# Norm chains in pieces, and a new order of the second block's attention, modulation and output

## What is computed

```python
mod = jax.nn.silu(c) @ w_ada[l] + b_ada[l]
sh1, sc1, g1, sh2, sc2, g2 = jnp.split(mod, N_MOD, axis=-1)
h = rms_norm(x, norm1_g[l]) * (1.0 + sc1[:, None]) + sh1[:, None]
z = h @ w_in[l]                      # q, k, v (512 each) and u (512) for the pools
a_out = diff_attention(q, k, v, lam, subln_g[l], lambda_init)
p_out = multiscale_pool(u, w_pool[l], pool_scale[l])
mix = jnp.concatenate([a_out, p_out], axis=-1) @ w_out[l]
x = x + g1[:, None] * mix
h = rms_norm(x, norm2_g[l]) * (1.0 + sc2[:, None]) + sh2[:, None]
y = hierarchical_moe(h, ...)
x = x + g2[:, None] * y
return rms_norm(x, final_g)
```

## Time and profile before

| | |
|---|---|
| median of 3 runs | 2242.56 us (2238.19 to 2245.31) |
| span of the profiled execution | 2239.7 us |
| TensorE matmul busy | 2032.3 us, 91% |
| TensorE weight load busy | 1722.9 us, 77% |
| VectorE busy | 1202.3 us, 54% |
| ScalarE busy | 902.2 us, 40% |
| HBM read | 496.03 MB, 222 GB/s over the span |

### The profile page before, as it was taken

How to read it: one execution, slowest core, us unless ns; L and a number is a source line. 1 busy time by engine, 2 the same in 40 slices (tenths; PEclk the granted TensorE clock), 3 DMA queues, 4 the chain that set the end, 5 groups by cost and what they waited for, 6 DMA issues and landing times.

```text
span 2239.7 us, 47727 instructions
## 1 busy us (share of the span) xinstructions
PE 2032.3 (91%) x20606; PEld 1722.9 (77%) x20606; DVE 1202.3 (54%) x2113; ACT 902.2 (40%) x1088; POOL 30.9 (1%) x61
## 2 busy tenths in 40 slices
PE   8999999989999999999999999999897767777775
PEld 7998858889999989988588899999776533343433
DVE  4887856388677557878563886775233200000001
ACT  5554533474555455545334755554312200000001
POOL 0000000000000000000000000000000000000000
PEclk9999999999999999999999999999998898878878
DMA  6554333445445554553334454556662699999996
GB/s 254 183 204 178 132 113 133 160 160 189 169 178 187 202 196 175 208 184 132 114 132 160 160 182 165 182 188 226 249 242 94 276 421 422 422 422 422 422 422 259
DMA packets 70920, 499.45 MB, mean 223 GB/s; under 512 B 8320, under 2 KB 8448, under 8 KB 12016
## 3 DMA queue, kind: packets, MB, share of 16 engines
q1 hardware_dynamic: 66240, 481.41, 56.2%
q0 software_dynamic: 4384, 14.75, 1.9%
q10 hardware_dynamic: 144, 1.05, 0.1%
HBM read 496.03 MB, written 1.15 MB: 222 GB/s over the span
## 4 chain that ended last, share of the span: by engine, by line
PE 69%; DMA 14%; DVE 6%; ACT 5%; SPq 3%; issue 2%; DVEq 0%; ACTq 0%
PE bank L863 25%; PE bank L868 12%; DMA ring<-stream 11%; PE bank L873 9%; DMA arena<-stream 4%; SPq L715 3%; PE bank L1102 3%; PE bank L806 2%; PE bank L851 2%; PE bank L818 2%; PE bank L1320 2%; PE bank L856 1%; PE bank L1217 1%; PE bank L1075 1%; PE bank L924 1%
## 5 line engine op out<-in xcount | busy, mean ns | idle before, releaser
L873 PE MATMUL bank<-u,ring 128*128 128x256 f32 x1152 | 256.2, 381 | 0.0
L2241 DVE TENSOR_TENSOR ring_r<-ring,weights_and_u_split 128x2048 fp32r<-128x2048 f32 x88 | 201.6, 2292 | 94.0 <-ACT weights_and_u_split L1680 90.3
L873 PEld LDWEIGHTS bank<-u,ring 128*128 128x128 f32 x1152 | 216.9, 190 | 30.2 <-issue 0.8
L2556 DVE COPY arena<-bank 128x128 f32<-128x128 f32 x32 | 9.3, 292 | 401.8 <-PE bank L1338 401.8
L868 PE MATMUL bank<-weights_and_u_split,ring_r 128*128 128x256 f32 x1592 | 208.9, 283 | 0.0
L1680 ACT ACTIVATE weights_and_u_split<-ring 128x2048 fp32r<-128x2048 f32 x88 | 167.8, 1908 | 96.5 <-PE bank L868 52.6
L863 PE MATMUL bank<-weights_and_u_split,hidden_and_weights_high 128*128 128x256 f32 x1600 | 202.1, 284 | 0.0
L863 PEld LDWEIGHTS bank<-weights_and_u_split,hidden_and_weights_high 128*128 128x128 f32 x1600 | 195.4, 192 | 4.7 <-issue 4.3
L868 PEld LDWEIGHTS bank<-weights_and_u_split,ring_r 128*128 128x128 f32 x1592 | 199.0, 192 | 0.0
L2241 DVE TENSOR_TENSOR ring_r<-ring,hidden_and_weights_high 128x2048 fp32r<-128x2048 f32 x60 | 137.0, 2287 | 33.5 <-ACT hidden_and_weights_high L1680 33.5
L1320 PE MATMUL bank<-ring,arena 128*32 128x256 f32 x1008 | 90.6, 489 | 58.9 <-DMA ring<-stream 58.9
(11 more groups left out here) (407 smaller groups left out, 3491.8 us busy)
## 6 DMA issues: line engine op xcount, KB each, us to landing
ring<-stream SPq DMA_DIRECT2D x329, 1024.0 KB, 4.8
arena<-stream SPq DMA_DIRECT2D x128, 1024.0 KB, 26.2
arena<-rows_scratch POOLq DMA_DIRECT2D x48, 256.0 KB, 4.1
h<-x_d ACTq DMA_DIRECT2D x1, 1024.0 KB, 5.5
out<-arena SPq DMA_DIRECT2D x1, 1024.0 KB, 3.9
con<-con_d SPq DMA_DIRECT2D x1, 976.5 KB, 12.6
arena<-con_d POOLq DMA_DIRECT2D x1, 848.0 KB, 7.1
par<-par_d POOLq DMA_DIRECT2D x2, 422.0 KB, 4.6
```

What stands on the lines that cost most here:

```text
L873: mm = pe.matmul(bank[:, c * S:(c + 1) * S], w[:, k, c * P:(c + 1) * P], x[:, k, :], start=(k == 0), stop=(k == KC - 1))
L2241: tt(ring_r[:, POS[k] % RING, :], w, high(k).bitcast(F32), ALU.subtract).then_inc(wlo_ok.sem, 1)
```

## The change

- Norms. `prime()` loads the set `natural_log_exp_and_others`, which has both Ln and Exp, in place of the small Ln. The sum of squares is made in four pieces (`norm_sum`) where the squares come one after the other: between the last units of a layer for the next layer's norm (`next_square`, `next_sum`), between the output units for the norm before the router, and behind each pair of additions at the end (`y2_fin` is raised for each pair). Where the set is loaded already, in `norm2(1)` and `norm2(2)`, nothing is loaded again.
- Start. x comes in four DMAs with a semaphore each, the table set is loaded before x is waited for, the first weight unit is split ahead of u (`parts` is an entry of its own behind `split 1`), silu(c) and the first ada pair come after the second "z" unit. The ring's first load waits for the second piece of x.
- Pairs of the first block. The first of a layer goes from the norm to behind "z" unit 1, the third from behind "bh" to the end of the layer, between the last sums.
- Second block. One ada pair ahead of the input units, the others at PAIR_AT. The input units come as q 0, k 0, v 0, pools, q 1, k 1, v 1, and scores, softmax, turns and values of heads 0 and 1 are put among them. Heads 2 and 3 follow with the pool halves of all four output units between, then the head norm and all four head halves. Output units use banks G0, G1, A0, A1, head sums bank G2.
- The five early expert units are asked for four units sooner. The output goes out in two halves.

The diff, cut to its core:

```diff
+        if n == OF["z"] + 1:
+            out += [ADA1, ADA1 + 1]
         elif n == OF["gh"] + 3:
             out += [ADA1 + 2, ADA1 + 3]
-        elif n == bh + 3:
-            out += [ADA1 + 4, ADA1 + 5]
+    return out + [ADA1 + 4, ADA1 + 5]
...
+WIN_AT = (2, 3, 6, 7, 10, 13, 14, 15)
+WIN_ORDER = (0, 2, 4, 6, 7, 1, 3, 5)
+PAIR_AT = (0, 4, 8, 11, 16, 18)
...
-        sched = [("norm", 0), ("ada", 0), ("ada_read", 0), ("split", 1), ("unit", 0), ("ada_cols", 0), ("lb", 0), ("split", 2), ("rows", 0)]
+        sched = [("norm", 0), ("split", 1), ("parts", 0), ("unit", 0), ("lb", 0), ("split", 2), ("rows", 0)]
...
             elif n >= pleg:
                 sched.append(("ple_add", n - pleg))
+                if n > pleg:
+                    sched.append(("next_sum", n - pleg - 1))
+                sched.append(("next_square", n - pleg))
+        sched += [("ada", 2), ("ada_read", 2), ("next_sum", 3), ("ada_cols", 2)]
...
-                    sp.wait_ge(x_in, 16)
+                    sp.wait_ge(x_in[1], 16)
...
-                early = n - B2 - WIN2 - 3
+                early = n - B2 - 5
...
-                sp.wait_ge(y2_fin, 2)
-                sp.dma_start(out, flat(0, KC)).then_inc(stored, 16)
-                sp.wait_ge(stored, 16)
+                for n in range(2):
+                    sp.wait_ge(y2_fin, 5 + n)
+                    sp.dma_start(out[:, n * 4 * S:(n + 1) * 4 * S], flat(4 * n, 4)).then_inc(stored, 16)
+                sp.wait_ge(stored, 32)
...
+            def norm_sum(lay, before, j):
+
+                pe.wait_ge(sq_ready.sem, sq_ready.at(lay, before + j + 1))
+                for c in (2 * j, 2 * j + 1):
+                    mm = pe.matmul(A[4][:, 0:S], ones, arena[:, SQ + c, :], start=(c == 0), stop=(c == KC - 1))
+                if j == 3:
+                    mm.then_inc(ss_ready.sem, 1)
...
             def prime():
 
-                act.activation(small[:, 255:256], eps[:, 0:1], ACT.Ln)
+                act.preload_act_table_set("natural_log_exp_and_others")
```

470 lines of the change are left out of this document (263 added, 207 removed).

## The result

The kernel after takes 2229.26 us in the median of 5 runs (2228.25 to 2233.54), beside 2239.28 for the kernel before (2238.19 to 2245.31): a ratio of 0.9946, with a 95% interval from 0.993 to 0.9962 (the intervals of all ratios below are of this kind). The profiled execution spans 2226.2 us, 13.5 less than before. That is faster, but by a third to under a half of the 30.4 us of my sum, and 0.26 us beyond the upper end of the range.

A forecast was written before the change was run, and what follows sets the result against it. TensorE was taken to bound the kernel up to the experts, the 422 GB/s stream within them. Gains of 2.3+5.5+7.1+11+4.5 = 30.4 us gave a span of 2209.3 and a median of 2212.2 us, range 2203 to 2229.

The forecast's parts named there:

- What bounds the kernel: Whole kernel: TensorE sets the pace up to the experts, then the weight stream at 422 GB/s, which the change leaves alone.
- The layers' norms: Boundary of layers 0 and 1: 0.5 us gained to 1/rms, 1.8 to the second z unit, 2.3 together; pairs cost nothing net.
- The start: Layer 0 up to the second z unit: earlier table load and x in pieces bring it to 24.1, gain taken as 5.5 us.
- Into the second block: Last gate product to first input unit: 14.7 us instead of 21.8, gain 7.1.
- Input units, attention, output: First input unit to router: 130.3 us instead of 141.4, gain 11, bounds 5 and 15.
- the 3 us "for switches": First input unit to router: allowance of 3 us because more short pieces mean more switches.
- the router's chain: Final chain to the router: loses the table load and most of the sums, 4.4 us idle stay.
- Rival (a): Attention: waits in the fixed orders replace those removed, at most 3 of the 11 us remain; 2220 us, chance 0.17.
- Rival (d): Input units: small attention pieces bring TensorE's clock down and it stays down; slower, 2269 us for eight units, chance 0.04.
- The end: Final norm and output: sums start sooner, products 3.7 us sooner, output halves 0.8; gain 4.5 us.
- rival (b): Seven norm and softmax chains: joint table set unused, Ln and Exp load their own; 18 us less gain, 2230 us, chance 0.05.

The follow-up runs named there:

- the four kernels named above: Of six kernels or repeats with nothing put behind "bh", those besides after and its repetition: 13.3 us for that stretch in layer 1, against 14.32 and 14.34.

## Why the prediction was wrong, step by step

**What bounds the kernel.** Right. The experts' stretch was the same to 0.3 us at 422 GB/s, and every microsecond by which the router came sooner was gained at the end.

**The layers' norms.** Here the prediction failed: of the 20.2 us between the forecast gain of 7.8 and the loss of 12.4, four places make 19.6.
- 7.5 us, in the trace of after (about 1 us less in the four kernels named above): "pair 2 leaves the full stretch by "bm", about -2.4". The stretch wasn't full. TensorE waits there for the turn's chain, and without the pair the clock falls, so the removal cost 0.8 and 1.9 us instead of saving 2.4 twice. The sum took a saving at the work's own duration in a place whose rows I had not read.
- 5.9 us: the boundary. Its own gain of 2.3 was right (2.4 with the parameters out of the way). But I had not asked what else u needs. The parameters are issued when h is complete; before, they landed 1.1 us ahead of need, 3.8 us after they were asked for, and no row showed a wait. 1/rms now came 2.4 us sooner after that moment, and with pair 2's two units asked for ahead of them they took 7.70 us (3.57 with pair 2 back behind "bh"): they became the last to arrive. The prediction has no word on GpSimd's queue.
- 4.7 us: pair 0 behind the second z unit. Its own 1.93 us were in the sum; the 3.4 us beyond them in layer 0 and 1.3 in layer 1 were ScalarE's list, the read and silu(c) behind a split that waits for the ring. The prediction looked at the ring's look-ahead for the second block ("four units ahead") and not here.
- 1.5 us: the lower clock near 292 us.

**The start.** The second z unit at 24.72 against 24.1, a gain of 5.5 against 5.5: right, though the start differs by 1 to 2 us between executions (23.4 to 25.9 in the kernels that share it), and worth nothing, because the moved pair and the 3.25 us of stall ahead of it took it back before the third z unit. A gain read at one milestone was not carried to the next.

**Into the second block.** The mechanism was right, the size not: with the 1.9 us of sums that lie ahead, 16.8 us instead of the forecast 14.7, a gain of 5.0 where I had 7.1. I had let the squares follow VectorE's products; they follow the read of pair 0 in ScalarE's list (1.1 us shown). Where the other 1 us comes from is open. One reading there was wrong without harm: 3 MB at 422 GB/s are over 7 us, not 5, but the pair (1601.02) waited for no transfer.

**Input units, attention, output.** The mechanism was right, the size too small: 125.6 us instead of 130.3, a gain of 15.8 where I had 11 and a bound of 15. TensorE's work is 118.9 us, and 114.9 + 4.3 made 119.2; the stop before the head halves is 3.73 (3.7). Two terms were mis-sized: the 3 us "for switches" between short pieces, of which 0.5 are there, and the router's chain, 2.46 instead of 4.4 (1736.01). Rival (a) found nothing. Rival (d) did not come either, the clock is 1.00 up to the head halves, but behind their stop of 3.73 us it fell for some 6 us and cost 1.7 us, for which the sum had no term.

**The end.** 14.8 instead of 19.6 us, a gain of 4.8 (4.5). The sums start 2.3 us after the first addition, not 1.5, and the two halves of the output bring 1.4 (from 4.4 to 3.0 us after the last product), where I took 0.8. The Trainium skill ("DMA: Bandwidth & Descriptors", Anatomy of one DMA) has a fixed cost of about 2.0 us for a transfer that GpSimd issues; worked out from it, the estimate in the prediction was 1.2. The output's transfers are issued by SyncE, and the trace is nearer to 1.2 than to 0.8.

**Rivals.** The time that came was that of rival (b), 2230, by coincidence: the joint set is used. Its worth, 8.5 us, is what the sum had taken for it (seven loads of 1.28, 9.0); the 18 of (b) had a second load in each chain, and that case did not come. None of my rivals had the first block as its place, and that is the fault of the range: it was made of the second block's uncertainties and gave the first block none.

## What to carry to other kernels

Work that leaves a place gains its duration only if the engine was the last to arrive there; where it was not, the work was free, and a filler may even keep TensorE's clock up. Ask it of every place that work leaves as well as of the place that it goes to. In lists that run in order, price an operation by what stands behind it: a read, silu(c) or a 0.16 us copy that waits for something held 3 to 5 us of other work here. And when a chain gets shorter, list every operand of its next step, transfers on quiet queues included, with the time at which each is there now.

## What the hardware showed that I had not expected

- The parameters, 422 KB on GpSimd's queue, took 7.70 us to land while the ring's units came in on SyncE's queue, and 3.57 us with pair 2's two units out of the way, which ended VectorE's wait 4.0 us sooner.
- TensorE's granted clock fell behind two idle pieces of 0.55 and 1.62 us among short pieces of work (16 products in 3.14 us instead of 2.08). Behind two of 1.94 and 1.7 us at the boundary of the layers a row unit took 5.27 to 6.29 us instead of 3.67. Work of no use in the place brought the clock back in both cases, behind "bh" with a shorter stretch as the result.
- In the second block the clock stayed at 1.00 for 100 us (1610.37 to 1711.00) with 1.1 us of idle time, but behind one piece of 3.73 us it was 0.66 and 0.76 over the next 6 us, although a long run of products followed it. The 48 products behind it took 12.31 us in 14 of 16 traces, 12.12 in one and 10.63 in one. One kernel can differ from itself: behind the same 2.10 us of idle time its first two input units took 14.41 us in one trace and 15.62 in another.
